# K-tile by K-tile or unit by unit: the order of the first two slabs in three weights of a fused two-block kernel

## The reference

```python
# block 1
u = rms_norm(h, mix_pre_g); proj = u @ w_in          # attention, convolution, gates
h = h + rms_norm(merged @ w_out, mix_post_g)
u = rms_norm(h, ffn_pre_g)
gate, up = split(u @ w_gate_up)                      # 2048 x 11264
h = h + rms_norm((silu(gate) * up) @ w_down, ffn_post_g)
# block 2, even layer
y = mixed(x @ ev_w_in) @ ev_w_out                    # ev_w_in is 2048 x 6144
x = layer_norm(ALPHA * x + y)
# block 2, odd layer: r, k, v, g projections, a recurrence over 256 steps, then
o = (group_norm(o) + bonus) * silu(xg @ w_g)
x = layer_norm(ALPHA * x + o @ w_o)
```

## Time and profile before

| | us |
|---|---|
| median of three runs | 2474.51 |
| span of the profiled execution | 2472.7 |
| PE busy (matmul) | 2433.6 |
| PE weight load busy | 2101.8 |
| DVE busy | 1605.8 |
| ACT busy | 1181.2 |
| POOL busy | 75.6 |
| PE's two waits at w_o | 2.3 and 2.5 |

### The profile page before, as it was taken

How to read it: one execution, slowest core, us unless ns; L and a number is a source line. 1 busy time by engine, 2 the same in 40 slices (tenths; PEclk the granted TensorE clock), 3 DMA queues, 4 the chain that set the end, 5 groups by cost and what they waited for, 6 DMA issues and landing times.

```text
span 2472.7 us, 38019 instructions
## 1 busy us (share of the span) xinstructions
PE 2433.6 (98%) x15334; PEld 2101.8 (85%) x15334; DVE 1605.8 (65%) x2159; ACT 1181.2 (48%) x1559; POOL 75.6 (3%) x98
## 2 busy tenths in 40 slices
PE   8999999999999999999999999999999999999997
PEld 7888888888888888888888788888888888887776
DVE  6888888775766566665444656676731676755576
ACT  5444554654544444444444455554545302455644
POOL 0000000000000000000000000000000201021000
PEclk9999999999999999999999999999999999999999
DMA  6665556565465656566665455555743456522463
GB/s 229 191 191 164 162 178 192 181 213 181 131 198 182 199 184 197 179 197 191 189 190 181 155 178 171 170 175 176 221 153 105 144 168 201 176 86 79 128 203 129
DMA packets 419888, 427.68 MB, mean 173 GB/s; under 512 B 25393, under 2 KB 414513, under 8 KB 418881
## 3 DMA queue, kind: packets, MB, share of 16 engines
q1 hardware_dynamic: 414880, 403.07, 51.7%
q0 software_dynamic: 4832, 22.19, 2.9%
HBM read 415.19 MB, written 9.96 MB: 172 GB/s over the span
## 4 chain that ended last, share of the span: by engine, by line
PE 91%; DVE 5%; ACT 2%; DMA 1%; issue 1%; SPq 0%; ACTq 0%; DVEq 0%
PE GP L1953 84%; PE SB L1953 7%; DVE wL L1103 1%; ACT wH L550 1%; DVE y L1103 1%; DMA raw<-w_in_dram 1%; DVE j L1103 1%; DVE x L1103 0%; DVE f L1109 0%; PE SB L1957 0%; DVE sq L1103 0%; DVE wide L1103 0%; DVE xB L1103 0%; ACT x L868 0%; PE GP L1957 0%
## 5 line engine op out<-in xcount | busy, mean ns | idle before, releaser
L1103 DVE TENSOR_TENSOR wL<-raw,wH 128x1024 fp32r<-128x1024 f32 x680 | 825.6, 1225 | 480.5 <-ACT wH L550 479.0
L550 ACT CAST wH<-raw 128x1024 fp32r<-128x1024 f32 x680 | 702.8, 1047 | 490.7 <-PE GP L1953 372.7
L1953 PE MATMUL GP<-u2B,wH 128*128 128x512 f32 x1408 | 442.2, 395 | 0.0
L1953 PE MATMUL GP<-uB,wH 128*128 128x512 f32 x1152 | 363.5, 397 | 0.0
L1953 PEld LDWEIGHTS GP<-u2B,wL 128*128 128x128 f32 x1408 | 264.1, 188 | 65.3 <-DVE u2B L1109 2.1
L1953 PE MATMUL GP<-u2B,wL 128*128 128x256 f32 x1408 | 277.8, 279 | 1.5 <-DVE u2B L1109 1.5
L1953 PEld LDWEIGHTS GP<-uB,wL 128*128 128x128 f32 x1152 | 216.7, 189 | 55.0 <-DVE wL L1103 4.2
L1953 PE MATMUL GP<-xB,wH 128*128 128x512 f32 x768 | 241.2, 395 | 0.0
L1953 PE MATMUL GP<-uB,wL 128*128 128x256 f32 x1152 | 232.7, 283 | 4.6 <-DVE wL L1103 3.8
L1953 PE MATMUL GP<-hB,wH 128*128 128x512 f32 x704 | 221.1, 395 | 0.0
L1953 PEld LDWEIGHTS GP<-u2B,wH 128*128 128x128 f32 x1408 | 214.3, 189 | 0.0
(11 more groups left out here) (413 smaller groups left out, 3123.5 us busy)
## 6 DMA issues: line engine op xcount, KB each, us to landing
raw<-w_gate_up_dram SPq DMA_DIRECT2D x352, 256.0 KB, 3.8
raw<-w_in_dram SPq DMA_DIRECT2D x288, 256.0 KB, 3.4
raw<-ev_w_in_dram SPq DMA_DIRECT2D x192, 256.0 KB, 3.4
raw<-w_down_dram SPq DMA_DIRECT2D x176, 256.0 KB, 3.4
raw<-w_out_dram SPq DMA_DIRECT2D x64, 256.0 KB, 3.8
raw<-ev_w_out_dram SPq DMA_DIRECT2D x64, 256.0 KB, 3.5
dw<-w_k_dram SPq DMA_DIRECT2D x64, 256.0 KB, 3.4
dw<-w_r_dram SPq DMA_DIRECT2D x64, 256.0 KB, 3.2
```

Source lines behind the costliest of these rows:

```text
L550: e.copy(wH[SLOT[i]], raw[k].rearrange("p (k n) -> p k n", k=4)).then_inc(s["hi"], 1)
L1103: return e.tensor_tensor(o, a, b, op)
L1953: return e.matmul(o, l, r, start=start, stop=stop, skip_group_check=True)
```

## The change

PE's `stream` is split into two helpers, the waits of a unit (`weights_of`) and one K-tile (`tile_of`). For three weights, the units up to the sixth are taken in pairs: K-tile k of the even unit (first slab), K-tile k of the odd unit (second slab), then k + 1. The waits of each unit stand before its own first K-tile. The seventh and eighth unit (K-tiles 12 to 15) keep the old order. `side(u)` for both units of a pair comes behind the whole pair. ACT, DVE, SP and POOL keep their programs. Eight semaphores of the two norms of block 1 are merged with their counterparts, with counts that go on (`POST`); the numbers of waits and increments stay.

```diff
+TILE_TURNS = ("w_gate_up", "ev_w_in", "w_o")
...
+POST = {"p1": 0, "p2": 1}
...
-                e.wait_ge(s["st1"], 4)
+                e.wait_ge(s["st"], 4)
...
-                for u in range(U0[name] + start * KUS[name], U1[name]):
+
+                def weights_of(u):
+
                     n, ku = UNITS[u]
-                    ps = GP[PAIR[n]]
                     before = [m for m in range(n) if PAIR[m] == PAIR[n]]
...
                     elif ku == 0 and before:
                         emptied(before[-1])
                     e.wait_ge(s["lo"], NTH[u] + 1)
...
+                def tile_of(u, k, behind_tile, t):
+                    n, ku = UNITS[u]
+                    ps, kt = GP[PAIR[n]], 4 * ku + k
+                    if n == first:
+                        ready(kt)
+                    for c in range(2):
+                        l = wL[SLOT[u]][:, k, c * P:(c + 1) * P]
+                        mm(ps[:, c, 0, :], l, xb[:, 0, kt, :], kt == 0, False)
+                    for c in range(2):
+                        h = wH[SLOT[u]][:, k, c * P:(c + 1) * P]
+                        ins = mm(ps[:, c], h, xb[:, :, kt, :], False, kt == 4 * KUS[name] - 1)
+                        if k == 3 and c == 1:
+                            ins.then_inc(s["unit"], 1)
...
+                for u in range(U0[name] + start * KUS[name], U1[name]):
+                    paired = name in TILE_TURNS and u < U0[name] + 2 * KUS[name] - 2
+                    if paired and u % 2 == U0[name] % 2:
+                        for k in range(4):
+                            for v in (u, u + 1):
+                                if k == 0:
+                                    weights_of(v)
+                                tile_of(v, k, None, 0)
+                    elif not paired:
+                        weights_of(u)
+                        t, behind_tile = turn_at(u) if turn else 0, turns_behind(u) if turn else None
+                        for k in range(4):
+                            t = tile_of(u, k, behind_tile, t)
                     if behind and u - 2 in ENDS and ENDS[u - 2] >= first:
                         behind(ENDS[u - 2] - first)
                     side(u)
```

More of the change, by code:

```diff
@@ L283 @@
 NORMED_BY = {step: n + 1 for n, step in enumerate(NORM_STEPS)}
+POST = {"p1": 0, "p2": 1}
 SUMMED = {"p1": 0, "p2": 6, "l1": 0, "l2": 8}
 SEMS = """vec xc0 xc1 xc2 xc3 cst bias raw0 raw1 raw2 raw3 raw4 hi lo unit lh ev eva val dr0 dr1 dr2 dr3 th tl
-sq1 st1 rt1 rs1 filled z ga aw cv at_vt at_vc at_pe at_act at_dve cn_pe cn_act cn_dve c_h c_l mg mh ml
-p1_sq p1_st p1_rt p1_f h1 sq2 st2 rt2 rs2 silu hm hh hl p2_sq p2_st p2_rt p2_f h2
+sq st rt rs filled z ga aw cv at_vt at_vc at_pe at_act at_dve cn_pe cn_act cn_dve c_h c_l mg mh ml
+p_sq p_st p_rt p_f h1 silu hm hh hl h2
 cnt wp0 wp1 sk_vt sk_vc sk_pe sk_act sk_dve xm_h xm_l pw pp pm pmx_h pmx_l
@@ L606, in scale1 @@
                     e.wait_ge(s[f"xc{q}"], 16)
-                    e.activation(squ[:, 4 * q:4 * q + 4, :], x[:, 4 * q:4 * q + 4, :], ACT.Square).then_inc(s["sq1"], 1)
+                    e.activation(squ[:, 4 * q:4 * q + 4, :], x[:, 4 * q:4 * q + 4, :], ACT.Square).then_inc(s["sq"], 1)
                     yield
-                e.wait_ge(s["st1"], 4)
-                e.activation(rsU, SB[0][:, 0:256], ACT.Sqrt, bias=C("eps")[:, 0:1], scale=1.0 / DM).then_inc(s["rt1"], 1)
+                e.wait_ge(s["st"], 4)
+                e.activation(rsU, SB[0][:, 0:256], ACT.Sqrt, bias=C("eps")[:, 0:1], scale=1.0 / DM).then_inc(s["rt"], 1)
             def u_tile(i):
@@ L713, in empty @@
                     to = sqb[:, 2 * (j % 2):2 * (j % 2) + 2, :] if j else total
-                    e.activation(to, o, ACT.Square).then_inc(s[key + "_sq"], 1)
+                    e.activation(to, o, ACT.Square).then_inc(s["p_sq"], 1)
                 return empty
@@ L723, in post_rt @@
             def post_rt(key):
-                e.wait_ge(s[key + "_st"], 2)
-                inverse_root(rsA, SB[0][:, 0:256], 0, 1.0 / DM, key + "_rt", 0)
+                e.wait_ge(s["p_st"], 2 * POST[key] + 2)
+                inverse_root(rsA, SB[0][:, 0:256], 0, 1.0 / DM, "p_rt", 2 * POST[key])
             def u2_tile(i):
@@ L736, in scale2 @@
                     e.wait_ge(s["h1"], 4 * q + 4)
-                    e.activation(sq2[:, 4 * q:4 * q + 4, :], x[:, 4 * q:4 * q + 4, :], ACT.Square).then_inc(s["sq2"], 1)
+                    e.activation(sq2[:, 4 * q:4 * q + 4, :], x[:, 4 * q:4 * q + 4, :], ACT.Square).then_inc(s["sq"], 1)
                     yield
@@ L741, in scale2 @@
                 e.preload_act_table_set("sqrt_and_others")
-                e.wait_ge(s["st2"], 4)
-                e.activation(rsU, SB[1][:, 0:256], ACT.Sqrt, bias=C("eps")[:, 0:1], scale=1.0 / DM).then_inc(s["rt2"], 1)
+                e.wait_ge(s["st"], 8)
+                e.activation(rsU, SB[1][:, 0:256], ACT.Sqrt, bias=C("eps")[:, 0:1], scale=1.0 / DM).then_inc(s["rt"], 1)
                 yield
@@ L1168, in scale1 @@
                     yield
-                e.wait_ge(s["rt1"], 1)
-                e.reciprocal(rsU, rsU).then_inc(s["rs1"], 1)
+                e.wait_ge(s["rt"], 1)
+                e.reciprocal(rsU, rsU).then_inc(s["rs"], 1)
             def u_tile(i):
@@ L1192, in empty_in @@
                 if n == N0["w_in"]:
-                    e.wait_ge(s["rs1"], 1)
+                    e.wait_ge(s["rs"], 1)
                 if sl < 8:
@@ L1313, in behind @@
                     if 0 < j < 7:
-                        e.wait_ge(s[key + "_sq"], j + 1)
+                        e.wait_ge(s["p_sq"], 8 * POST[key] + j + 1)
                         if j > 1:
@@ L1320, in post_rs @@
             def post_rs(key):
-                e.wait_ge(s[key + "_rt"], 2)
+                e.wait_ge(s["p_rt"], 2 * POST[key] + 2)
             def post_tile(i, fb, gname, key, done):
-                stt(fb[:, i, :], fb[:, i, :], V(gname, i), rsA, ALU.mult, ALU.mult).then_inc(s[key + "_f"], 1)
-                e.wait_ge(s[key + "_f"], i + 1)
+                stt(fb[:, i, :], fb[:, i, :], V(gname, i), rsA, ALU.mult, ALU.mult).then_inc(s["p_f"], 1)
+                e.wait_ge(s["p_f"], 16 * POST[key] + i + 1)
                 tt(x[:, i, :], x[:, i, :], fb[:, i, :], ALU.add).then_inc(s[done], 1)
@@ L1338, in scale2 @@
                     yield
-                e.wait_ge(s["rt2"], 1)
-                e.reciprocal(rsU, rsU).then_inc(s["rs2"], 1)
-                e.wait_ge(s["rs2"], 1)
+                e.wait_ge(s["rt"], 2)
+                e.reciprocal(rsU, rsU).then_inc(s["rs"], 1)
+                e.wait_ge(s["rs"], 2)
                 scaled_gu(0)
@@ L1986, in stream @@
                     e.wait_ge(s["lo"], NTH[u] + 1)
[L1987 to L2004, removed]
+                def tile_of(u, k, behind_tile, t):
[11 more added lines that the diff above has]
+                            ins.then_inc(s["unit"], 1)
+                        if turn:
+                            for _ in range(behind_tile[2 * k + c]):
+                                turn(t)
+                                t += 1
+                    return t
@@ L2040, in kept_busy, with scale @@
                     mm(to[:, 0:256], tile[:, 0:P], tile[:, 0:256], True, True)
-            def scale(x_, psum, key, late):
+            def scale(x_, psum, first, late):
                 yield
@@ L2048, in scale @@
                         e.wait_ge(s["cst"], 16)
-                    e.wait_ge(s["sq" + key], q + 1)
-                    stat(psum, [x_[:, 4 * q + i, :] for i in range(4)], q == 0, q == 3).then_inc(s["st" + key], 1)
+                    e.wait_ge(s["sq"], first + q + 1)
+                    stat(psum, [x_[:, 4 * q + i, :] for i in range(4)], q == 0, q == 3).then_inc(s["st"], 1)
                     yield
@@ L2109, in behind @@
                         e.wait_ge(s["sq_sum"], SUMMED[key] + 6)
-                        stat(SB[0][:, 0:256], [total[:, i, :] for i in range(2)], True, False).then_inc(s[key + "_st"], 1)
+                        stat(SB[0][:, 0:256], [total[:, i, :] for i in range(2)], True, False).then_inc(s["p_st"], 1)
                     if j == 7:
-                        e.wait_ge(s[key + "_sq"], 8)
-                        stat(SB[0][:, 0:256], [sqb[:, 2 + i, :] for i in range(2)], False, True).then_inc(s[key + "_st"], 1)
+                        e.wait_ge(s["p_sq"], 8 * POST[key] + 8)
+                        stat(SB[0][:, 0:256], [sqb[:, 2 + i, :] for i in range(2)], False, True).then_inc(s["p_st"], 1)
                 return behind
@@ L2405, in ready_gated @@
                     e.wait_ge(s["oy_l"], kt // 2 + 1)
-            tasks = {"scale1": scale(squ, SB[0][:, 0:256], "1", False), "attention0": attention(0),
+            tasks = {"scale1": scale(squ, SB[0][:, 0:256], 0, False), "attention0": attention(0),
                      "attention1": attention(1), "conv_norm": conv_norm(),
```

(2 more changed lines are left out.)

## The result

The changed kernel takes 2479.26 us (median of 20 runs, 2476.99 to 2481.46), the kernel before 2474.49 us (20 runs, 2473.44 to 2477.13): +4.8 us, ratio 1.0017, 95% interval 1.0011 to 1.0023. The forecast was +2.9 us, 2477.4, range 2474.6 to 2480.2. The profiled execution spans 2477.3 us, 4.6 more than before.

A forecast was written before the change was run, and what follows sets the result against it. TensorE (PE), busy nearly all of the span, was taken as the bound, so only its few waits could give time. Terms 0 (w_gate_up), 0 (ev_w_in), 2.1 (w_o), 0.8 (clock) gave +2.9 us: 2477.4 us, range 2474.6 to 2480.2.

The forecast's parts named there:

- the case that I held the likeliest: Whole kernel: no clock effect anywhere at one end, the forecast's clock cost at the other, +2.1 to +3.7 us; chance 0.65.
- rival B: Lower clock in w_gate_up, ev_w_in and longer in w_o: +6.1 us, 2480.6; chance 0.14 for more than 4.95.
- one of my signs of being wrong: The forecast is wrong if the granted clock falls in more than one of w_gate_up, ev_w_in and w_o.
- w_gate_up, gain 0: At w_gate_up, PE gets ahead 1.6 us but waits 2.4 us for ACT's square, unmoved behind DVE's full chain: 0.
- ev_w_in, gain 0: At ev_w_in, PE gets ahead by up to 2 us but waits longer for K-tile 14, released at 1404.58: 0.
- w_o, +2.1 us: At w_o, the wait for gv comes after one tile, not four, leaving three tiles of 0.70 us behind it.
- an upper bound of +0.8: Clock behind w_o's wait for gv: bounds -1.6 (no fall) to +0.8 us (as at the kernel's start), taken as 0.
- the delayed casts: In w_o, later even-unit ends delay casts, transfers and x's reload by about 2 us: cost nothing; without cover, 2.1 us more.
- The clock at w_gate_up, +0.8: The new single 2.4 us wait at w_gate_up may lower the clock: bounds 0 and +1.6 us, middle taken.
- A: Arrival waits in w_gate_up and ev_w_in really won: about -1.5 us with w_o's cost, 2473.0 us; chance 0.08.
- D: As a rival: w_o's release comes later or weights fall behind, a second 2.1 us, 2479.5; chance 0.05.
- E: Order makes no difference in w_o: without the clock fall, -1.6 cancels most of +2.1, 2475 us; chance 0.08.

The follow-up runs named there:

- the run with all units paired: All eight units of w_gate_up and ev_w_in paired, w_gate_up's sums later, w_o in old order, against the kernel before: 2474.47 against 2474.45 us.
- the run with fillers: Old order everywhere, with five filler matmuls in each of w_o's two waits, against the kernel before: 2473.61 against 2474.45 us.
- the change with the clock kept: The whole change plus five filler matmuls before w_gate_up's wait for ACT's square, against the kernel before: 2477.09 us, +2.6 us.
- w_o from the third unit: Only w_o paired, its first two units in the old order, against the kernel before: 2474.85 against 2474.88 us.

## Which steps of the forecast held, and which were too small

The time, 2479.26 us, lies in the range, near its upper end, and 1.9 us above the forecast. The mechanism was right: the waits moved and weren't won, and the cost is the one wait in w_o and the clock. But +4.8 us is more than the upper end of the case that I held the likeliest, +2.1 to +3.7, and it lies where rival B puts two of its three falls, +4.5 to +5.3, of which I gave 0.14 to more than 4.95. The range held because it reached into B. And one of my signs of being wrong came about by its letter: the granted clock was low in two of the three places. I had put that sign badly, since the forecast itself kept the low clock in w_o.

**w_gate_up, gain 0:** right, by its mechanism. PE got to the sum 1.6 us sooner (10.5 against 12.1 us to the 16th tile) and waited 2.2 us, forecast 2.4 and 2.2 in two places, for a square that didn't move.

**ev_w_in, gain 0:** right. K-tile 14 holds PE to 0.01 us at the same place. I had missed the 0.82 us for the odd unit's weights, which that wait covers here; when I uncovered it, in the run with all units paired, waits of this kind kept the gain away.

**w_o, +2.1 us:** the mechanism is right, the term too small. The changed kernel's trace gives +2.9 for D: 2.1 for the three tiles, 0.5 for a longer stay at the lower clock, and 0.33 for the third slab's wait on the first slab's evacuation. For the clock I took 0 with an upper bound of +0.8; the four traces with w_o's first pair changed give 0.48, 0.80, 0.96 and 0.28, never 0 and once more than the bound. The idle time before the release I had put at 4.8 us; by my own rows it is 2.45 + 3 x 0.70 = 4.5, and the traces have 3.86 to 4.55. The third slab's wait came in two of these four traces. I had cost the delayed casts at nothing because no tile waits for them in the trace of before. But that trace has the slow stretch in it; when that goes, as in the run with fillers, the same wait appears with 1.1 us. An absent wait didn't mean that there was room.

**The clock at w_gate_up, +0.8:** mis-sized. I halved a term that either comes or doesn't; in the changed kernel's profiled execution, and again in the second one, it came, with 1.6 us each time. The medians give 2.2 us between the change with and without fillers. With w_gate_up alone it didn't come in the one trace, and the median didn't move. The parts alone add up to 2.4 us (+3.1, -0.1 and -0.55), together they are +4.8. A larger share of falls in the whole change would explain it, but with one trace for each kernel and intervals of 2.2 us it isn't shown, and why it should be so is open.

**The rivals.** A is out: no arrival wait was won. B came in part: the fall at w_gate_up and more low clock in w_o, but never a fall at ev_w_in in the traces. D came in small, 0.33 us. E didn't come: w_o's cost stayed in every kernel with its first pair changed.

The warning of the Trainium skill ("TensorE: Matmul & The Clock Gate", Why this matters for your kernels) about idle time between bursts of matmuls deserved more weight, and the traces agree with its direction: four waits of 0.2 to 0.7 us never let the clock fall in a trace here, the one of 2.2 us that replaced them did in two of three executions profiled without fillers, and filler work in the wait took the loss away. They don't agree with its bound, which I had left out: the page warns only of gaps longer than this one. Nor do my two rows, 2.27 and 2.45 us, mark a limit: 2.20 and 2.19 us let the clock fall and 2.18 didn't, and at w_o's start a whole tile at the full clock followed a wait of 2.38 us in the change with the clock kept (granted clock 1.00 over its first 0.55 us).

## What to carry to other kernels

Before you reorder an engine's work to remove waits on a producer, follow the producer's chain to the next point where the engine needs it: if the producer is full until there, the waits only move. Interleaving two streams brings every resource of the second one, its weights and its output buffer, forward to the first step; look up when each is free. Short waits spread out may be cheaper than the same time in one piece. Where one long wait must stay, matmuls on constants that fit into it can keep the clock up; here they cost nothing on the path.

## What the hardware showed that I had not expected

The lower clock was free where PE would have waited anyway: where it fell before or among w_o's four covered tiles (granted clock 0.55 in w_o from the third unit, 0.54 in w_gate_up alone), it was at 1.00 right after the release, and the 1.6 us were not paid there. And a fall that is paid can hide another wait: keeping the clock up in w_o brought 0.85 us in the median and 0.2 in its trace, not 1.6, until the evacuation behind it was moved too.
